# A two-block transformer kernel on one core: gate and up products with the two parts of the input side by side, and the norm's factors on GpSimd

## The chip, the cores and the metric

The program runs on one core of one Trainium2 chip. The metric is the device time of one execution in microseconds (us); the medians of several executions are compared.

## The reference, cut to what matters

Twelve stages work on a residual of 256 tokens by 1024 features in float32: attention of several kinds, a recurrent and a retention mixer, cross attention, and, six times, a SwiGLU feed-forward layer. Each stage is

```
x = x + rms_norm(stage(rms_norm(x, g_pre)), g_post)
swiglu(x, w_gate, w_up, w_down) = (silu(x @ w_gate) * (x @ w_up)) @ w_down     # 1024 -> 2816 -> 1024
```

The change lies in the six feed-forward stages, in the two products with `w_gate` and `w_up`.

## The kernel before

**Products in parts.** TensorE multiplies in fp32r. To keep float32 accuracy each operand is split: `whi` is the weight rounded to fp32r (ScalarE, `act_hi`, L304) and `wlo = raw - whi` (VectorE, `dve_lo`, L311); `xh` and `xl` are the two parts of the normed input, feature-major, `[128, 8, 256]` each. A product is the sum of three: `whi*xh`, `whi*xl`, `wlo*xh` (`mm3`, L243 to L245 and, by operand order, L250 to L252).

**The weight stream.** All weights come as 301 chunks of 128x2048 floats (1 MB each) through three slots: SyncE loads `raw` slot j when the `wlo` of the chunk that was there is done (`w_lo`), ScalarE makes `whi` when TensorE has used the slot (`w_used`), VectorE makes `wlo` when `whi` is there (`w_hi`). In chunk c's body both are made for chunk c+3. One chunk of gate and up holds a 128-column tile of each.

**A feed-forward stage** has 22 chunks of gate and up and 11 of the down product. `slices_pe` (L633, L639) does chunks 0 and 1 while the residual still comes in; `proj_pe` does 20 chunks of 48 products of 256 columns into one of three PSUM banks `pj` (gate in columns 0 to 255, up in the rest). The norm's factors (one for each token, `rP`) are applied behind the product:

- VectorE, for each chunk: L882 `GU = pj * rP` (frees the bank, `pj_free`); `dve_lo`; L887 `A = (TH + 1) * gate`; L890 `M = A * up / 2`; L893, the low part of M.
- ScalarE, for each chunk: `act_hi`; L905 `TH = tanh(gate / 2)`; L907, the high part of M (`own(c)`, `hi2`).
- GpSimd has no part in it; it works a few small operations between stages, and some in the attention of stages 0 and 9.

`GU`, `TH`, `A` and `M` have one buffer each, and each engine takes its instructions strictly in the order written. The down product (L250 to L252, 512 columns) begins behind chunk 21. The bodies of chunks 2 and on run in hardware loops of three chunks (`chunk_loop`). The PSUM banks `acc` hold the transposed residual at the start of a stage and the down product's sums at its end; between the two they are free.

Of the kernel before, what the change touches and what calls it, by code (L numbers as in the profile page):

```python
# [8 lines left out]
P = 128  # L9
D = 1024  # L10
T = 256
# [72 lines left out]
def build_program(nc, stages, wstream, xin, xtok, memin, memtok, vecs_d, gains_d, consts_d, rpb, small, out):  # L84
    NCH = n_chunks(stages)
    with ExitStack() as ctx:
# [5 lines left out]
        def sem(name):  # L92
            if name not in sems:
# [4 lines left out]
        NORM = {"sq": 2, "hi": KT, "lo": KT, "mv": 1, "rs": 1, "bc": 1, "rb": 1}  # L98
        attn = lambda units, groups, H=1: {**{n: units for n in ("s", "sm", "pn", "pt", "pts", "pv")}, "p": H * units,
                                           "od": groups}  # L100
        ADDS = {"ffn": {n: FT for n in ("th", "a", "m", "hi2", "lo2")}, "na": {**attn(8, 8, 4), "oh": 8},
                "dil": {**attn(16, 8, 2), "oh": 8, "pt": 32, "pts": 32}, "xa": {**attn(4, 4, 2), "oh": 4}, "dsa": attn(8, 8, 2), "rwrt": {}}
        base, count = {}, {}

# [21 lines left out]

        xt = sb("xt", [P, 2, D])
        x_at = nc.sbuf_base
        xh = sb("xh", [P, KT, T], F32R)
        xl = sb("xl", [P, KT, T], F32R)  # L130
        sb("space", [P, 16])
        raw = sb("raw", [P, 3, CHUNK])
        w_at = nc.sbuf_base
# [724 lines left out]


        def ffn(tag, s, nxt):  # L860
            sh = FS - KT * T - 5 * T
            GU = F0[:, sh:sh + 512]
            TH = F0[:, sh + 512:sh + 768]
            A = F0[:, sh + 768:sh + 1024]
            M = F0[:, sh + 1024:sh + 1280]

            def own(c):
                return AR[:, c, :] if isinstance(c, int) else AR[:, bass.ds(c, 1), :].rearrange("p o t -> p (o t)")

            def pe_f(pe, w):  # L870
                def tiles(c, j, bank, slot):
                    tile_fm(bank, 0, slot)
                    return tile_fm(bank, 1, slot)
                slices_pe(pe, w)
                proj_pe(pe, w, 1, tiles)
                proj_pe(pe, w, FT - 3, tiles)
                out_pe(pe, w, FT, FT, tag, "lo2", nxt, alternate=True)

            def dve_f(dve, w):
                def body(c, g, gs, it, p, ps):  # L880
                    dve.wait_ge(w_used, g + 1)
                    nc.vector.tensor_tensor(GU.rearrange("p (a t) -> p a t", a=2),  # L882
                                            pj[ps][:, :].rearrange("p (a t) -> p a t", a=2),
                                            rP[:, None, :].to_broadcast([P, 2, T]), ALU.mult).then_inc(pj_free, 1)
                    dve_lo(dve, g, gs)
                    dve.wait_ge(*at(tag, "th", c + 1))
                    nc.vector.scalar_tensor_tensor(A, TH, 1.0, GU[:, 0:T], ALU.add, ALU.mult)\  # L887
                        .then_inc(sg(tag, "a"), 1)
                    dve.wait_ge(*at(tag, "a", c + 1))
                    nc.vector.scalar_tensor_tensor(M, A, 0.5, GU[:, T:2 * T], ALU.mult, ALU.mult)\  # L890
                        .then_inc(sg(tag, "m"), 1)
                    dve.wait_ge(*at(tag, "hi2", c + 1))
                    nc.vector.tensor_tensor(own(c + FT), M, own(c).bitcast(F32), ALU.subtract)\  # L893
                        .then_inc(sg(tag, "lo2"), 1)
                chunk_loop(dve, w, FT, body, peel=2, is_proj=True)
                out_dve(dve, w, FT)

            def act_f(act, w):
                def body(c, g, gs, it, p, ps):
                    if not isinstance(c, int) or c != 1:  # L900
                        act_hi(act, g, gs, it, c)
                    if isinstance(c, int) and c == 0:
                        act_hi(act, g + 1, (g + 1) % 3, (g + 1) // 3, c)
                    act.wait_ge(pj_free, p + 4)
                    nc.scalar.activation(TH, GU[:, 0:T], ACT.Tanh, scale=0.5).then_inc(sg(tag, "th"), 1)  # L905
                    act.wait_ge(*at(tag, "m", c + 1))
                    nc.scalar.activation(own(c), M, ACT.Copy).then_inc(sg(tag, "hi2"), 1)  # L907
                chunk_loop(act, w, FT, body, peel=2, is_proj=True)
                out_act(act, w, s, FT)
            return pe_f, dve_f, act_f  # L910


        mem_hi, mem_lo = AR[:, 16:24, :], AR[:, 24:32, :]
# [61 lines left out]
        def mixer(tag, kind, s, nxt):  # L975
# [267 lines left out]

            def load(sp):
                if na:
                    sp.dma_start(MK, c_dram("na_mask")).then_inc(Mx("tm"), 16)
                    sp.dma_start(NB[:, 0, :], rpb[0, :, :]).then_inc(Mx("tl0"), 16)
                else:
                    sp.dma_start(DM.rearrange("p a n -> p (a n)"), c_dram("dist")).then_inc(Mx("tl"), 16)

            def pool_f(gp):
                if not na:
                    return
                def made(x, n):
                    x.then_inc(Mx("made"), 1)
                    gp.wait_ge(Mx("made"), n)

                def masked(ps_):
                    gp.wait_ge(Mx(f"tl{ps_}"), 16)
                    b = NB[:, ps_, :].rearrange("p (a c) -> p a c", c=T)  # L1260
                    made(nc.gpsimd.tensor_tensor(b, b, MK[:, None, :].to_broadcast([P, 4, T]), ALU.add), BIASED[ps_])

                def mixed(ps_):
                    VB = VBs[ps_ % 3]
                    gp.wait_ge(pj_free, 3 + NCP * (ps_ + 1))
                    if ps_ == 3:
                        gp.wait_ge(*at(tag, "pv", 2))
                    moves = ((1, 3, slice(0, 32)), (1, 0, slice(32, 64)), (1, 0, slice(64, 128)),
                             (2, 3, slice(0, 64)), (2, 3, slice(64, 96)), (2, 0, slice(96, 128)))
                    for n, (i, j, rows) in enumerate(moves):  # L1270
                        made(nc.gpsimd.tensor_copy(VB[rows, :, i, :], VB[rows, :, j, :]), MIXED[ps_] - 5 + n)

                gp.wait_ge(Mx("tm"), 16)
                masked(0)
                masked(1)
                mixed(0)
                mixed(1)
                masked(2)
                mixed(2)
                masked(3)  # L1280
                mixed(3)
# [1467 lines left out]
        @block.scalar  # L2749
        def _(act):  # L2750
            w = Walk()
            act.wait_ge(sem("power"), 1)
            nc.scalar.activation(rsc[:, 0:1], power[:, 0:1], ACT.Copy)
            act.wait_ge(sem("in_vecs"), 16)
            for i in range(2):
                act.wait_ge(x_in[i], 16)
                for k in range(4 * i, 4 * i + 4):
                    pre_hi(act, "s0pre", "na0_pre", False, k)
                act.wait_ge(w_raw[i], 16)
                nc.scalar.activation(whi[:, i, :], raw[:, i, :], ACT.Copy).then_inc(w_hi, 1)  # L2760
            act.wait_ge(x_in[2], 16)
            pre_sq(act, "s0pre")
            act.wait_ge(w_raw[2], 16)
            nc.scalar.activation(whi[:, 2, :], raw[:, 2, :], ACT.Copy).then_inc(w_hi, 1)
            for s, kind, idx, fns in plan:
                fns[2](act, w)
                post_act(act, w, f"s{s}post", out_banks(kind))
                if s + 1 < len(plan):
                    nx = plan[s + 1]
                    pre_act(act, w, f"s{s + 1}pre", f"{nx[1]}{nx[2]}_pre", nx[1] == "dil")  # L2770
                    if len(nx[3]) > 3:
                        nx[3][3](act)

        @block.vector
        def _(dve):
            w = Walk()
            nc.vector.memset(AR[:, 0:2, :].bitcast(F32), 0.0).then_inc(sem("zeroed"), 1)
            nc.vector.memset(nt[:, :], 0.0).then_inc(pj_free, 3)
            dve.wait_ge(pj_free, 3)
            dve.wait_ge(sem("in_vecs"), 16)  # L2780
            for i in range(2):
# [21 lines left out]
        @block.gpsimd  # L2803
        def _(gp):
            nc.gpsimd.memset(power[:, :], -0.5).then_inc(sem("power"), 1)
            gp.wait_ge(sem("power"), 1)
            stats_pool(gp, "s0pre", rsc[:, 2:4], 8)
            for s, kind, idx, fns in plan:
                if kind == "dsa":
                    gp.wait_ge(sem(f"s{s}_mv"), 1)  # L2810
                    nc.gpsimd.tensor_tensor(nt[:, 8:12], nt[:, 0:4], power[:, 0:4], ALU.pow)\
                        .then_inc(sem(f"s{s}_rs"), 1)
                    fns[4](gp)
                if kind in ("rwrt", "na"):
                    fns[4](gp)
                if kind in ("dsa", "rwrt"):
                    mem_pool(gp, f"s{s + 1}m")
                post_pool(gp, f"s{s}post")
                if s + 1 < len(plan):
                    stats_pool(gp, f"s{s + 1}pre", rsc[:, 2:4], 8)  # L2820

        @block.tensor
        def _(pe):
# [4 lines left out]
                for _ in range(n):  # L2828
                    nc.tensor.matmul(mb[:, 0:T], AR[:, 0, 0:P], AR[:, 1, :], start=True, stop=True)

            pe.wait_ge(sem("zeroed"), 1)
            pe.wait_ge(x_in[0], 16)
            warm(26)
            pe.wait_ge(sem("in_cst"), 16)
# [206 lines left out]
```

## Time and profile before

| | us |
|---|---|
| median of 3 runs | 1929.08 (1928.88 to 1930.92) |
| the profiled execution, its own time | 1927.48 |
| its span | 1925.7 |
| granted TensorE clock, mean | 0.995 |

The span is what the rows below are read from; 1.8 us of the execution lie around it. Engines: PE is TensorE, DVE VectorE, ACT ScalarE, POOL GpSimd. A busy share is over the whole span and mixes all stages.

### The profile page before, as it was taken

Reading aid. Unit: us, or ns where it says so; the run is one execution under the profiler, and the core shown is the slowest. Engines: PE = TensorE matmul, PEld = TensorE weight load, DVE = VectorE, ACT = ScalarE, POOL = GpSimd, SP = SyncE. Lnnn points to the kernel's source line nnn. Section 1 sums busy time; section 2 is a strip of 40 time slices with the busy share of each in tenths; the row PEclk is TensorE's granted clock in tenths of the full one; section 3 lists DMA queues with packets and bytes.
Section 4 is the critical chain, followed back from the end, with each engine's and each line's share of the span. In section 5 each row is a group of like instructions: output and inputs, shape, how many; then the busy total and the mean of one; then the engine's idle time right before and its main releaser. Section 6 shows DMA issues by size and latency. Waiting matters only on the chain.

```text
span 1925.7 us, 38585 instructions
## 1 busy us (share of the span) xinstructions
PE 1864.5 (97%) x15800; PEld 1761.9 (91%) x15800; DVE 1339.8 (70%) x1814; ACT 920.9 (48%) x1255; POOL 85.0 (4%) x104
## 2 busy tenths in 40 slices
PE   8999999999989999999999999999999999899998
PEld 8989989999979998999998888999899988799997
DVE  6867756766777775776677677777577667677774
ACT  5554445444454444444436454444444444555442
POOL 2300000000000000000000010000000003100000
PEclk9999999999999999999999999999999999999999
DMA  7445564443525564556541223556455652354553
GB/s 293 154 165 197 185 237 183 176 177 132 182 93 187 186 229 174 188 183 233 216 173 53 112 94 148 189 185 228 174 191 183 234 206 110 121 186 153 177 204 131
DMA packets 50099, 338.13 MB, mean 176 GB/s; under 512 B 6080, under 2 KB 7232, under 8 KB 10560
## 3 DMA queue, kind: packets, MB, share of 16 engines
q1 hardware_dynamic: 45072, 319.74, 45.8%
q10 hardware_dynamic: 4912, 16.71, 2.4%
q8 instruction: 90, 1.47, 0.3%
q14 instruction: 25, 0.20, 0.0%
HBM read 335.38 MB, written 1.05 MB: 175 GB/s over the span
## 4 chain that ended last, share of the span: by engine, by line
PE 62%; DVE 13%; ACT 11%; issue 9%; POOL 1%; ACTq 1%; DVEq 0%; POOLq 0%
PE pj L243 9%; PE pj L245 9%; PE pj L244 9%; ACT whi L304 9%; PE acc L250 5%; PE acc L251 5%; PE acc L252 5%; DVE wlo L311 4%; PE pj L633 3%; PE pj L250 2%; PE pj L251 2%; PE pj L252 2%; PE pj L639 2%; DVE F L890 2%; DVE F L887 1%
## 5 line engine op out<-in xcount | busy, mean ns | idle before, releaser
L311 DVE TENSOR_TENSOR wlo<-raw,whi 128x2048 fp32r<-128x2048 f32 x285 | 651.8, 2291 | 238.8 <-ACT whi L304 237.7
L243 PE MATMUL pj<-xh,whi 128*128 128x256 f32 x2672 | 739.7, 277 | 1.3 <-DVE wlo L311 0.5
L244 PE MATMUL pj<-xl,whi 128*128 128x256 f32 x2672 | 734.8, 275 | 0.0
L245 PE MATMUL pj<-xh,wlo 128*128 128x256 f32 x2672 | 734.8, 275 | 0.0
L304 ACT ACTIVATE whi<-raw 128x2048 fp32r<-128x2048 f32 x298 | 567.9, 1912 | 331.2 <-PE acc L252 142.8
L243 PEld LDWEIGHTS pj<-xh,whi 128*128 128x128 f32 x2672 | 512.8, 192 | 6.3 <-issue 2.2
L245 PEld LDWEIGHTS pj<-xh,wlo 128*128 128x128 f32 x2672 | 513.0, 192 | 0.0
L244 PEld LDWEIGHTS pj<-xl,whi 128*128 128x128 f32 x2672 | 512.9, 192 | 0.1
L250 PE MATMUL acc<-whi,AR 128*128 128x512 f32 x656 | 253.9, 387 | 3.8 <-DVE AR L1449 3.3
L251 PE MATMUL acc<-whi,AR 128*128 128x512 f32 x656 | 249.6, 381 | 0.0
L252 PE MATMUL acc<-wlo,AR 128*128 128x512 f32 x656 | 249.4, 380 | 0.0
L907 ACT ACTIVATE AR<-F 128x256 f32 (+1 forms) x132 | 55.2, 418 | 375.3 <-DVE F L890 375.3
L250 PEld LDWEIGHTS acc<-whi,AR 128*128 128x128 f32 x656 | 128.3, 196 | 24.8 <-DVE wlo L311 7.1
L252 PEld LDWEIGHTS acc<-wlo,AR 128*128 128x128 f32 x656 | 128.4, 196 | 14.1
L251 PEld LDWEIGHTS acc<-whi,AR 128*128 128x128 f32 x656 | 128.4, 196 | 13.1
L893 DVE TENSOR_TENSOR AR<-F,AR 128x256 f32 (+1 forms) x132 | 56.2, 426 | 101.4 <-ACT AR L907 101.4
L882 DVE TENSOR_TENSOR F<-pj,rP 128x512 f32<-128x512 f32 x132 | 90.5, 686 | 1.4
L250 PE MATMUL pj<-whi,xh 128*128 128x256 f32 x288 | 80.2, 279 | 1.8 <-issue 1.7
L633 PE MATMUL pj<-xh,whi 128*128 128x256 f32 x320 | 80.1, 288 | 0.1
L251 PE MATMUL pj<-whi,xl 128*128 128x256 f32 x288 | 79.2, 275 | 0.0
L252 PE MATMUL pj<-wlo,xh 128*128 128x256 f32 x288 | 79.2, 275 | 0.0
L633 PE MATMUL pj<-xh,wlo 128*128 128x256 f32 x320 | 76.0, 275 | 0.0
(398 smaller groups left out, 2196.3 us busy)
## 6 DMA issues: line engine op xcount, KB each, us to landing
raw<-in_wstream SPq DMA_DIRECT2D x301, 1024.0 KB, 4.8
F<-in_gains ACTq DMA_DIRECT2D x12, 512.0 KB, 4.3
XM<-in_memtok ACTq DMA_DIRECT2D x2, 1024.0 KB, 4.9
XM<-in_memin ACTq DMA_DIRECT2D x2, 1024.0 KB, 7.8
F<-in_rpb ACTq DMA_DIRECT2D x3, 512.0 KB, 3.8
F<-in_small ACTq DMA_DIRECT2D x1, 1536.0 KB, 9.4
F<-in_xin SPq DMA_DIRECT2D x2, 512.0 KB, 6.4
xt<-in_xtok SPq DMA_DIRECT2D x1, 1024.0 KB, 11.7
```

Source lines behind the costliest of these rows:

```text
L243: nc.tensor.matmul(o, wh, k_hi, start=first, stop=False, skip_group_check=True)
L244: nc.tensor.matmul(o, wh, k_lo, start=False, stop=False, skip_group_check=True)
L245: return nc.tensor.matmul(o, wl, k_hi, start=False, stop=last, skip_group_check=True)
L250: nc.tensor.matmul(o, k_hi, wh, start=first, stop=False, skip_group_check=True)
L251: nc.tensor.matmul(o, k_lo, wh, start=False, stop=False, skip_group_check=True)
L252: return nc.tensor.matmul(o, k_hi, wl, start=False, stop=last, skip_group_check=True)
L304: nc.scalar.activation(whi[:, gs, :], raw[:, gs, :], ACT.Copy).then_inc(w_hi, 1)
L311: nc.vector.tensor_tensor(wlo[:, gs, :], raw[:, gs, :], whi[:, gs, :].bitcast(F32), ALU.subtract).then_inc(w_lo, 1)
L633: nc.tensor.matmul(o, a[:, (w.g + c) % 3, wk], woven(xh[:, k, :]), start=k == 0 and half == 0 and i == 0, stop=False, skip_group_check=True)
L882: nc.vector.tensor_tensor(GU.rearrange("p (a t) -> p a t", a=2), pj[ps][:, :].rearrange("p (a t) -> p a t", a=2), rP[:, None, :].to_broadc ...
L893: nc.vector.tensor_tensor(own(c + FT), M, own(c).bitcast(F32), ALU.subtract)\
L907: nc.scalar.activation(own(c), M, ACT.Copy).then_inc(sg(tag, "hi2"), 1)
```

## The change

For chunks 2 to 19 of each feed-forward stage (18 of 22), with `xh` and `xl` now neighbours in one tile `xhl`:

- TensorE multiplies each `whi` block once, with both parts of the input, as one product of 512 columns (128 of them for each half of each part, interleaved as before), and then adds `wlo*xh` in columns 0 to 255. Gate goes to bank `pj[ps]`, up to bank `acc[ps]`; each bank then holds the main sum in columns 0 to 255 and the `whi*xl` sum in columns 256 to 511.
- ScalarE copies the two `whi*xl` sums to `LOW` (two new copies of 256 columns, ahead of `act_hi`).
- VectorE adds each bank's main sum and `LOW` into `SUM` (two additions of 256 columns in place of the multiplication of 512), and then frees the banks.
- GpSimd multiplies `SUM` by `rP` into `GU` (one operation of 512 columns, both inputs in SBUF) and signals `gu`; tanh waits for that.
- `dve_lo` in these bodies is that of the chunk before (`g - 1`), so `wlo` of chunk c+2 is made in body c, not that of c+3. Body 20 makes two.

Beside it, two waits on small start-up semaphores are merged into others (`tm` into `tl0`, `zeroed` into `pj_free`).

```diff
+        xhl = sb("xhl", [P, 2, KT, T], F32R)
+        xh, xl = xhl[:, 0, :, :], xhl[:, 1, :, :]
...
+            def wide(c):
+                return not isinstance(c, int) or 2 <= c < FT - 2
...
+                def both_parts(c, g, gs, it, p, ps):
+                    pe.wait_ge(w_lo, g + 1)
+                    pe.wait_ge(pj_free, p + 1)
+                    for half, bank in enumerate((pj[ps], acc[ps])):
+                        for k in range(KT):
+                            wk = slice((half * KT + k) * P, (half * KT + k + 1) * P)
+                            nc.tensor.matmul(bank[:, :], whi[:, gs, wk],
+                                             xhl[:, :, k, :].rearrange("p s (a b) -> p s b a", a=2),
+                                             start=k == 0, stop=False, skip_group_check=True)
+                            last = nc.tensor.matmul(bank[:, 0:T], wlo[:, gs, wk], woven(xh[:, k, :]),
+                                                    start=False, stop=k == KT - 1, skip_group_check=True)
+                    last.then_inc(w_used, 1)
                 slices_pe(pe, w)
-                proj_pe(pe, w, 1, tiles)
-                proj_pe(pe, w, FT - 3, tiles)
+                chunk_loop(pe, w, FT - 4, both_parts, peel=3, is_proj=True)
+                proj_pe(pe, w, 2, tiles)
+                pe.wait_ge(pj_free, 3 + p0 + FT - 2)
...
             def dve_f(dve, w):
                 def body(c, g, gs, it, p, ps):
                     dve.wait_ge(w_used, g + 1)
-                    nc.vector.tensor_tensor(GU..., pj..., rP..., ALU.mult).then_inc(pj_free, 1)
-                    dve_lo(dve, g, gs)
+                    if wide(c):
+                        dve.wait_ge(*at(tag, "ls", c - 1))
+                        for half, bank in enumerate((pj[ps], acc[ps])):
+                            hh = slice(half * T, (half + 1) * T)
+                            x = nc.vector.tensor_tensor(SUM[:, hh], bank[:, 0:T], LOW[:, hh], ALU.add)
+                        x.then_inc(pj_free, 1)
+                    else:
+                        nc.vector.tensor_tensor(GU..., pj..., rP..., ALU.mult).then_inc(pj_free, 1)
+                    if wide(c) or c == FT - 2:
+                        dve_lo(dve, g - 1, (gs + 2) % 3)
+                    if not wide(c) and c != 1:
+                        dve_lo(dve, g, gs)
...
             def act_f(act, w):
                 def body(c, g, gs, it, p, ps):
+                    if wide(c):
+                        act.wait_ge(w_used, g + 1)
+                        for half, bank in enumerate((pj[ps], acc[ps])):
+                            x = nc.scalar.activation(LOW[:, half * T:(half + 1) * T], bank[:, T:2 * T], ACT.Copy)
+                        x.then_inc(sg(tag, "ls"), 1)
...
-                    act.wait_ge(pj_free, p + 4)
+                    if wide(c):
+                        act.wait_ge(*at(tag, "gu", c - 1))
+                    else:
+                        act.wait_ge(pj_free, p + 4)
...
+            def pool_f(gp):
+                def body(c, g, gs, it, p, ps):
+                    gp.wait_ge(pj_free, 3 + p0 + 2 + c + 1)
+                    nc.gpsimd.tensor_tensor(GU..., SUM..., rP..., ALU.mult).then_inc(sg(tag, "gu"), 1)
+                chunk_loop(gp, Walk(), FT - 4, body)
```

## Rows read from the trace of the kernel before

**Rows 1.** The page: span, and each engine's busy time, share and instructions.
```profile
span 1925.7 us, 38585 instructions
...
PE 1864.5 (97%) x15800; PEld 1761.9 (91%) x15800; DVE 1339.8 (70%) x1814; ACT 920.9 (48%) x1255; POOL 85.0 (4%) x104
```

**Rows 2.** Timeline of TensorE, first feed-forward stage: start, duration, engine, line.
```profile
135.62 0.38 PE L243 MATMUL pj<-xh,whi 128*128 128x256 f32 x1
...
171.24 0.28 PE L243 MATMUL pj<-xh,whi 128*128 128x256 f32 x1
...
173.91 0.28 PE L243 MATMUL pj<-xh,whi 128*128 128x256 f32 x1
...
243.25 0.49 PE L250 MATMUL acc<-whi,AR 128*128 128x512 f32 x1
...
245.73 0.38 PE L252 MATMUL acc<-wlo,AR 128*128 128x512 f32 x1
...
248.32 0.38 PE L252 MATMUL acc<-wlo,AR 128*128 128x512 f32 x1
248.72 0.49 PE L250 MATMUL acc<-whi,AR 128*128 128x512 f32 x1
```

**Rows 3.** Timeline of VectorE, one chunk of the same stage and the next one's beginning.
```profile
167.84 0.68 DVE L882 TENSOR_TENSOR F<-pj,rP 128x512 f32<-128x512 f32 x1
168.96 2.29 DVE L311 TENSOR_TENSOR wlo<-raw,whi 128x2048 fp32r<-128x2048 f32 x1 [0.44 <-ACT whi L304]
171.17 0.42 DVE L887 SCALAR_TENSOR_TENSOR F<-F 128x256 f32<-128x256 f32 x1
171.62 0.42 DVE L890 SCALAR_TENSOR_TENSOR F<-F 128x256 f32<-128x256 f32 x1
172.85 0.43 DVE L893 TENSOR_TENSOR AR<-F,AR 128x256 f32 x1 [0.80 <-ACT AR L907]
173.19 0.68 DVE L882 TENSOR_TENSOR F<-pj,rP 128x512 f32<-128x512 f32 x1
```

**Rows 4.** Timeline of ScalarE, the same stage: the seam between two bodies, twice.
```profile
172.17 0.42 ACT L907 ACTIVATE AR<-F 128x256 f32 x1 [2.95 <-DVE F L890]
172.50 1.90 ACT L304 ACTIVATE whi<-raw 128x2048 fp32r<-128x2048 f32 x1
...
177.64 0.42 ACT L907 ACTIVATE AR<-F 128x256 f32 x1 [2.94 <-DVE F L890]
178.15 1.92 ACT L304 ACTIVATE whi<-raw 128x2048 fp32r<-128x2048 f32 x1
```

**Rows 5.** Groups by shape: a ScalarE copy of 256 columns out of PSUM.
```profile
L2639 ACT ACTIVATE PTb<-pj 128x256 f32<-128x256 f32 x5 | 1.9, 384 | 0.4
```

**Rows 6.** Timeline of GpSimd and of VectorE where both work, two places.
```profile
19.97 2.37 POOL L1261 TENSOR_TENSOR F<-F 128x1024 f32<-128x1024 f32 x1 [1.01 <-DMA F<-in_rpb]
...
20.20 4.28 DVE L321 TENSOR_TENSOR wlo<-raw,whi 128x2048 fp32r<-128x2048 f32 x1 [2.09 <-ACT whi L2764]
...
1641.93 1.82 POOL L1868 TENSOR_TENSOR F<-F 128x256 f32<-128x256 f32 x1
...
1641.95 1.22 DVE L317 TENSOR_TENSOR wlo<-raw,whi 128x1024 fp32r<-128x1024 f32 x1
```

**Rows 7.** One line of GpSimd: count, shortest, median and longest in ns.
```profile
L1868 POOL TENSOR_TENSOR F<-F x4: 730/732/1816, 1623.5 to 1641.9; 128x256 f32<-128x256 f32 x4
```

**Rows 8.** The page's DMA issues: KB each, median us to landing.
```profile
raw<-in_wstream SPq DMA_DIRECT2D x301, 1024.0 KB, 4.8
```

**Rows 9.** TensorE in stage 9: its timeline, then a window with its granted clock.
```profile
1647.66 0.56 PE L716 MATMUL acc<-cst,Sb 128*128 128x128 f32 x2 [1.91 <-DVE Sb L770]
...
1648.00:1650.00 2.00, 2.00 (x11) 0.50 0.82 315
```

More of the change, by code:

```diff
@@ L100, in build_program @@
                                            "od": groups}
-        ADDS = {"ffn": {n: FT for n in ("th", "a", "m", "hi2", "lo2")}, "na": {**attn(8, 8, 4), "oh": 8},
+        ADDS = {"ffn": {**{n: FT for n in ("th", "a", "m", "hi2", "lo2")}, "gu": FT - 4, "ls": FT - 4}, "na": {**attn(8, 8, 4), "oh": 8},
                 "dil": {**attn(16, 8, 2), "oh": 8, "pt": 32, "pts": 32}, "xa": {**attn(4, 4, 2), "oh": 4}, "dsa": attn(8, 8, 2), "rwrt": {}}
@@ L128, in build_program @@
         x_at = nc.sbuf_base
-        xh = sb("xh", [P, KT, T], F32R)
-        xl = sb("xl", [P, KT, T], F32R)
+        xhl = sb("xhl", [P, 2, KT, T], F32R)
+        xh, xl = xhl[:, 0, :, :], xhl[:, 1, :, :]
         sb("space", [P, 16])
@@ L860, in ffn @@
         def ffn(tag, s, nxt):
[L861 to L865, printed above, removed]
+            sh = FS - KT * T - 9 * T
+            SUM = F0[:, sh:sh + 512]
+            GU = F0[:, sh + 512:sh + 1024]
+            TH = F0[:, sh + 1024:sh + 1280]
+            A = F0[:, sh + 1280:sh + 1536]
+            M = F0[:, sh + 1536:sh + 1792]
+            LOW = F0[:, sh + 1792:sh + 2304]
+            p0 = sum(proj_chunks(kind_) for kind_, _ in stages[:s])
             def own(c):
                 return AR[:, c, :] if isinstance(c, int) else AR[:, bass.ds(c, 1), :].rearrange("p o t -> p (o t)")
+            def wide(c):
+                return not isinstance(c, int) or 2 <= c < FT - 2
             def pe_f(pe, w):
+                assert w.p == p0
                 def tiles(c, j, bank, slot):
@@ L881, in body @@
                     dve.wait_ge(w_used, g + 1)
-                    nc.vector.tensor_tensor(GU.rearrange("p (a t) -> p a t", a=2),
-                                            pj[ps][:, :].rearrange("p (a t) -> p a t", a=2),
-                                            rP[:, None, :].to_broadcast([P, 2, T]), ALU.mult).then_inc(pj_free, 1)
-                    dve_lo(dve, g, gs)
+                    if wide(c):
[5 more added lines that the diff above has]
+                    else:
+                        nc.vector.tensor_tensor(GU.rearrange("p (a t) -> p a t", a=2),
+                                                pj[ps][:, :].rearrange("p (a t) -> p a t", a=2),
+                                                rP[:, None, :].to_broadcast([P, 2, T]), ALU.mult).then_inc(pj_free, 1)
+                    if wide(c) or c == FT - 2:
+                        dve_lo(dve, g - 1, (gs + 2) % 3)
+                    if not wide(c) and c != 1:
+                        dve_lo(dve, g, gs)
                     dve.wait_ge(*at(tag, "th", c + 1))
@@ L909, in act_f @@
                 out_act(act, w, s, FT)
-            return pe_f, dve_f, act_f
+            def pool_f(gp):
+                def body(c, g, gs, it, p, ps):
+                    gp.wait_ge(pj_free, 3 + p0 + 2 + c + 1)
+                    nc.gpsimd.tensor_tensor(GU.rearrange("p (a t) -> p a t", a=2), SUM.rearrange("p (a t) -> p a t", a=2),
+                                            rP[:, None, :].to_broadcast([P, 2, T]), ALU.mult).then_inc(sg(tag, "gu"), 1)
+                chunk_loop(gp, Walk(), FT - 4, body)
+            return pe_f, dve_f, act_f, None, pool_f
         mem_hi, mem_lo = AR[:, 16:24, :], AR[:, 24:32, :]
@@ L1245, in load @@
                 if na:
-                    sp.dma_start(MK, c_dram("na_mask")).then_inc(Mx("tm"), 16)
+                    sp.dma_start(MK, c_dram("na_mask")).then_inc(Mx("tl0"), 16)
                     sp.dma_start(NB[:, 0, :], rpb[0, :, :]).then_inc(Mx("tl0"), 16)
@@ L1258, in masked @@
                 def masked(ps_):
-                    gp.wait_ge(Mx(f"tl{ps_}"), 16)
+                    gp.wait_ge(Mx(f"tl{ps_}"), 16 if ps_ else 32)
                     b = NB[:, ps_, :].rearrange("p (a c) -> p a c", c=T)
@@ L1271, in mixed @@
                         made(nc.gpsimd.tensor_copy(VB[rows, :, i, :], VB[rows, :, j, :]), MIXED[ps_] - 5 + n)
-                gp.wait_ge(Mx("tm"), 16)
                 masked(0)
@@ L2770, in _ @@
                     pre_act(act, w, f"s{s + 1}pre", f"{nx[1]}{nx[2]}_pre", nx[1] == "dil")
-                    if len(nx[3]) > 3:
+                    if len(nx[3]) > 3 and nx[3][3]:
                         nx[3][3](act)
@@ L2776, in _ @@
             w = Walk()
-            nc.vector.memset(AR[:, 0:2, :].bitcast(F32), 0.0).then_inc(sem("zeroed"), 1)
-            nc.vector.memset(nt[:, :], 0.0).then_inc(pj_free, 3)
+            nc.vector.memset(AR[:, 0:2, :].bitcast(F32), 0.0).then_inc(pj_free, 1)
+            nc.vector.memset(nt[:, :], 0.0).then_inc(pj_free, 2)
             dve.wait_ge(pj_free, 3)
@@ L2813, in _ @@
                     fns[4](gp)
-                if kind in ("rwrt", "na"):
+                if kind in ("rwrt", "na", "ffn"):
                     fns[4](gp)
@@ L2829, in warm @@
                     nc.tensor.matmul(mb[:, 0:T], AR[:, 0, 0:P], AR[:, 1, :], start=True, stop=True)
-            pe.wait_ge(sem("zeroed"), 1)
+            pe.wait_ge(pj_free, 3)
             pe.wait_ge(x_in[0], 16)
```

## The prediction

> **What bounds the kernel now.** I read the page's first part, then the timelines of the four engines inside one feed-forward stage. On the page TensorE is busy 97% of the span, VectorE 70%, GpSimd 4% [rows 1]: TensorE's time is the kernel's time, and GpSimd looks free. The timelines qualify this. TensorE runs chunks 2 to 21 from 135.62 to 243.25, 107.63 us or 5.38 a chunk, without a visible gap [rows 2]. VectorE and ScalarE form a closed ring beside it: `act_hi` is queued behind `own(c)`, `dve_lo` needs `act_hi`, A and M follow, and `own(c+1)` needs M. From one L907 to the next it is 172.17 to 177.64, 5.47 us [rows 4], a little more than TensorE's chunk; the three-deep buffers absorb the difference until the down product, where TensorE waits about 0.2 us for a weight's low part (248.32 to 248.72, against a step of 0.216) [rows 2]. So two things decide what the change is worth: TensorE's columns, and whether the ring, which it lengthens, still fits.
>
> **TensorE's part.** Inside a chunk 24 products of 256 columns take 171.24 to 173.91, 0.1113 each; 12 of 512 take 245.73 to 248.32, 0.2158 each [rows 2]. A wide chunk has 16 products of 512 and 16 of 256 in place of 48 of 256: it saves 16 x (0.2226 - 0.2158) = 0.11 us and takes 5.38 - 0.11 = 5.27. Over 18 x 6 = 108 chunks that is 11.8 us at most; nothing, if the interleaved wide product costs twice the narrow one. The Trainium skill (TensorE: Matmul & The Clock Gate, "Back-to-back issue gap") gives columns / 2.4 + 2.5 ns, which is 109.2 and 215.8 ns: the trace agrees at 512 and not at 256, and by the page the saving would be an estimated 4.5 us. Neither enters the sum below, because there TensorE isn't what is late.
>
> **The ring after the change.** The program order on each engine now makes one loop: ScalarE copies LOW (c+1) only behind `own(c)`, VectorE adds only behind LOW, GpSimd multiplies behind the additions, tanh waits for GpSimd, A for tanh, M for A, `own` for M. I add it up from the start of `own`:
>
> - `own` to the first copy 0.33 (172.17 to 172.50) [rows 4]; second copy 0.33 later; it lasts 0.38 [rows 5], and with 0.04 for the hand-over the first addition starts at 1.08. VectorE itself is ready at 1.02 (0.68 to L893, 0.34 more to the next) [rows 3], so it isn't later.
> - Additions of 256 columns: no longer than the 0.42 of the other 256-column operations, next start after 0.34 [rows 3]. Second addition 1.42 to 1.84; `dve_lo`, which waits for nothing now, starts at 1.76 and lasts 2.29, to 4.05.
> - GpSimd is released at 1.84, starts at about 1.90, and finds VectorE's L311 running. What then happens is the heart of this prediction. At 20.20 the VectorE subtraction (two SBUF inputs, elsewhere 2.29 [rows 3]) took 4.28 while GpSimd's 2.37 us operation from 19.97 was under way: it ended 2.14 after GpSimd did. At 1641.93 a GpSimd operation that otherwise takes 0.73 [rows 7] took 1.82 beside a VectorE subtraction of the same kind, and ended 0.58 behind it [rows 6]. So the one that comes second does practically all its work after the other's end, except some 0.15 us. That is no slow-down in proportion but an exclusion. The Trainium skill says the same (SBUF — State Buffer, "SBUF: two separate sides"): the port pair shared by VectorE and GpSimd is locked for the whole instruction by whoever starts first, where VectorE reads two SBUF inputs and GpSimd reads SBUF. The trace agrees with its 4.28 and 1.82. It is the rule that speaks against this change.
> - GpSimd's price for 512 columns: from 256 at 0.73 [rows 7] and 1024 at 2.37 [rows 6] a line gives 1.28; the bounds are half the large one, 1.19, and twice the small one, 1.46. Behind the lock it ends at 4.05 + 1.28 - 0.15 = 5.18.
> - tanh at 5.23, 0.40 long; A at 5.66; M 0.45 later; `own` 0.55 after M (171.62 to 172.17) [rows 3, 4]: 6.66. The hardware loop's branch adds 0.18 every third chunk (0.51 against 0.33) [rows 4], 0.06 on average: 6.72.
>
> The ring takes 6.72 us, TensorE's wide chunk 5.27. TensorE will idle 1.45 us in each.
>
> **One stage.** Count from 0, TensorE's start of chunk 2 (135.62 in the trace). Chunk 2 ends at 5.27, LOW and the additions begin (first addition 6.08), and `dve_lo` of chunk 4 ends at 9.05. From there the low part of chunk h, without which TensorE doesn't begin it, comes at 9.05 + 6.72 (h - 4): chunk 21 starts at 9.05 + 17 x 6.72 = 123.3. The down product needs `wlo` of chunk 22, made in body 20: `own(19)` is 2.61 after that start, L882 1.02 more, the subtraction some 0.6 behind L882 and 2.29 long, 6.5 in all (TensorE is through with chunk 21 at 5.38 and waits). The down product starts at 129.8, against 107.63 before: +22.2, less the 0.2 that TensorE waited there before, which the body's second `dve_lo` now covers. That is +22.0 us a stage, +132 for six.
>
> Costed at nothing: `act_hi` (1.9) lies under the wait for GpSimd; if that wait went it would still lie under `dve_lo`. The weight loads are asked for one body later, since SP waits for `w_lo`; the load for chunk c+3 is issued at the end of `dve_lo` in body c-2 and used at `act_hi` in body c, 2 x 6.72 - 3.05 = 10.4 us later, and takes 4.8 [rows 8]. Behind GpSimd's new wait nothing is queued until the stage's end (`post_pool`). The merged start-up semaphores: two waits, under 0.1 us either way. The `acc` banks are free in these chunks; the wait ahead of the down product is for an addition two chunks old.
>
> **Sum.** 1927.5 + 132 = 2059.5 for the profiled execution; that lies 1.6 below the median of 1929.1, so the median comes to 2061, 6.8% slower.
>
> **Rivals.**
>
> - *GpSimd comes first.* If the wait on `w_hi` holds `dve_lo` back by 0.2 us, GpSimd takes 1.90 to 3.18, and `dve_lo` ends 2.14 later, at 5.32; tanh is then covered, `own` follows at 6.24, with the branch 6.30. Stage: 6.08 + 4.24 + 17 x 6.30 + 5.4 = 122.8, +15.2, or +91 in all: 2020. Against it: VectorE starts the next instruction 0.34 behind a 0.42 us one [rows 3], ahead of its semaphore. Chance 0.13.
> - *No exclusion (the other side: faster).* If VectorE and GpSimd overlap, GpSimd is done at 3.18 and tanh before `dve_lo` ends; A at 3.97, M 4.42, `own` 4.97, with the branch 5.03, below 5.27. TensorE sets the pace, 0.11 us less a chunk, and its small wait goes: -13, 1916. It decides once the ring falls under about 5.4; the exclusion is worth 1.7 of 6.72, so nearly all of it has to be absent. For it: the rows of the exclusion are of other shapes, and GpSimd's are rough. Chance 0.11.
> - *No exclusion, and the interleaved wide product costs two narrow ones.* No gain: 1929. Chance 0.05.
> - *The clock.* TensorE fell to its lower level (granted 0.50) after 1.91 us of idling [rows 9]. The gaps here are 1.45, of a kind that repeats. One fall in each stage costs about 5.27 - 1.45 = 3.8 us, or 23 in all (2084); one in every third chunk 36 x 3.8 = 137 (2198). Against it: it lasted two windows and the gap before was longer. Chance 0.08.
>
> **The numbers.** The forecast has 0.63. Its own range: GpSimd at 1.19 or 1.46 moves the ring by -0.09 or +0.18, and 0.05 more on each of four hand-overs whose register waits I could not read adds 0.2; 17 x 6 rings make that -9 to +39: 2052 to 2100. With GpSimd first (2020, and its own bound of -9) and single falls of the clock inside, 2010 to 2105 holds about 8 in 10. A difference of 0.2% is about what the runs can tell from no change. Faster by more than that 0.11, within it 0.06, slower 0.83.
>
> **What would show it.** In the changed profile: L311 at 2.29 and, beside it, GpSimd's new line at about 3.3 us each (1.28 if there is no exclusion), or, with GpSimd first, GpSimd at 1.28 and L311 at 3.5; tanh's idle time ended by GpSimd; the period of a VectorE addition 6.7; TensorE waiting 1.4 us a chunk for `wlo` and its busy share down to about 91%; products of 512 in a step of 0.216; no change in other stages. I am wrong if the period is 5.3 with GpSimd's line short, and wrong in size if the period is right but TensorE's clock row shows half levels, or if the GpSimd line takes well over 1.5 net of the lock.

## The result, and the profile after

The changed kernel takes 2062.81 us (median of 4 runs, 2061.72 to 2064.42) against 1929.16 before: a ratio of 1.0691, 95% interval 1.0673 to 1.071. It is 6.9% slower; the forecast was 2061.

The page of the changed kernel, beside [rows 1]; PE is TensorE, DVE VectorE, ACT ScalarE. The last two lines are from its list of costly groups (engine, operation, output and inputs, shape, count | busy us, mean ns | idle time before it and what ended it):

```profile
span 2060.8 us, 35796 instructions
...
PE 1871.9 (91%) x14072; PEld 1702.4 (83%) x14072; DVE 1348.4 (65%) x1922; ACT 991.7 (48%) x1471; POOL 436.0 (21%) x212
...
PE 43%; issue 29%; POOL 12%; DVE 8%; ACT 3%; POOLq 0%; ACTq 0%; DVEq 0%
...
L955 POOL TENSOR_TENSOR F<-F,rP 128x512 f32<-128x512 f32 x108 | 351.1, 3251 | 422.9 <-DVE F L909 422.9
L889 PE MATMUL pj<-xhl,whi 128*128 128x512 f32 x864 | 298.8, 393 | 110.1 <-DVE wlo L311 109.8
```

TensorE's busy time barely moved (1864.5 to 1871.9), while its share fell from 97% to 91%: of the 135 us of span, 128 are idling of TensorE. The wide product's line now waits 109.8 us for VectorE's low part, where TensorE's lines before waited for next to nothing, and GpSimd, which had no part in the feed-forward stages, carries 12% of the chain that ended last (the chain is followed back from the last instruction of the run). No engine is full. What grew is a chain through several of them.

That chain can be read off three timelines of one chunk. GpSimd first, then VectorE (beside [rows 3]), then ScalarE (beside [rows 4]):

```profile
165.61 3.25 POOL L955 TENSOR_TENSOR F<-F,rP 128x512 f32<-128x512 f32 x1 [3.63 <-DVE F L909]
172.36 3.25 POOL L955 TENSOR_TENSOR F<-F,rP 128x512 f32<-128x512 f32 x1 [3.50 <-DVE F L909]
```

```profile
164.78 0.43 DVE L909 TENSOR_TENSOR F<-pj,F 128x256 f32<-128x256 f32 x1 [0.21 <-ACT F L936]
165.12 0.41 DVE L909 TENSOR_TENSOR F<-acc,F 128x256 f32<-128x256 f32 x1
165.45 2.28 DVE L311 TENSOR_TENSOR wlo<-raw,whi 128x2048 fp32r<-128x2048 f32 x1
169.34 0.43 DVE L920 SCALAR_TENSOR_TENSOR F<-F 128x256 f32<-128x256 f32 x1 [1.61 <-ACT F L946]
169.80 0.43 DVE L923 SCALAR_TENSOR_TENSOR F<-F 128x256 f32<-128x256 f32 x1
171.18 0.43 DVE L926 TENSOR_TENSOR AR<-F,AR 128x256 f32 x1 [0.95 <-ACT AR L948]
171.53 0.42 DVE L909 TENSOR_TENSOR F<-pj,F 128x256 f32<-128x256 f32 x1
```

```profile
168.89 0.42 ACT L946 ACTIVATE F<-F 128x256 f32<-128x256 f32 x1 [2.50 <-POOL F L955]
170.37 0.42 ACT L948 ACTIVATE AR<-F 128x256 f32 x1 [1.06 <-DVE F L923]
170.69 0.37 ACT L936 ACTIVATE F<-pj 128x256 f32<-128x256 f32 x1
```

The reader is to see one thing: the subtraction L311 starts at 165.45 and ends at 167.73, with its usual 2.28; GpSimd's product starts at 165.61, 0.16 later, and ends at 168.86, that is 1.13 behind the subtraction. It does not run beside it. tanh (L946) starts 0.03 after GpSimd's end, A (L920) when tanh is done, M, the high part (L948), and only then ScalarE's copies (L936) for the next chunk. VectorE stands idle for 1.61 us in the middle of its own ring. From the first `dve_lo` of the stage, at 144.83, to that of body 19, at 259.71, there are 17 periods of 6.76 us (forecast 6.72). The other five feed-forward stages run a little faster, 6.65 to 6.67 us from addition to addition; over all six the mean is 6.67. Why the first is slower stays open.

### The profile page after: what moved, and what is told of

Read it like the earlier page. It is cut to its first block, busy times and chain, and to the rows that moved or that the text cites. A ratio compares the mean times of both kernels' runs of the same rounds, so it can differ in the third digit from the quotient of the medians.

```text
span 2060.8 us, 35796 instructions
## 1 busy us (share of the span) xinstructions
PE 1871.9 (91%) x14072; PEld 1702.4 (83%) x14072; DVE 1348.4 (65%) x1922; ACT 991.7 (48%) x1471; POOL 436.0 (21%) x212
## 3 DMA queue, kind: packets, MB, share of 16 engines
q8 instruction: 92, 1.51, 0.3%
## 4 chain that ended last, share of the span: by engine, by line
PE 43%; issue 29%; POOL 12%; DVE 8%; ACT 3%; POOLq 0%; ACTq 0%; DVEq 0%
POOL F L955 11%; PE acc L250 6%; PE acc L252 6%; PE acc L251 6%; PE pj L243 4%; PE pj L245 4%; PE pj L244 4%; DVE wlo L311 2%; PE pj L250 2%; PE pj L252 2%; PE pj L251 2%; ACT whi L304 1%; PE pj L633 1%; PE mb L729 1%; PE acc L703 1%
## 5 line engine op out<-in xcount | busy, mean ns | idle before, releaser
L311 DVE TENSOR_TENSOR wlo<-raw,whi 128x2048 fp32r<-128x2048 f32 x285 | 650.8, 2288 | 188.5 <-ACT whi L304 187.7
L955 POOL TENSOR_TENSOR F<-F,rP 128x512 f32<-128x512 f32 x108 | 351.1, 3251 | 422.9 <-DVE F L909 422.9
L889 PE MATMUL pj<-xhl,whi 128*128 128x512 f32 x864 | 298.8, 393 | 110.1 <-DVE wlo L311 109.8
L889 PEld LDWEIGHTS pj<-xhl,whi 128*128 128x128 f32 x864 | 163.0, 189 | 159.2 <-issue 132.8
L889 PE MATMUL acc<-xhl,whi 128*128 128x512 f32 x864 | 288.8, 382 | 0.0
L243 PE MATMUL pj<-xhl,whi 128*128 128x256 f32 x944 | 264.6, 280 | 12.9 <-DVE wlo L311 12.8
L244 PE MATMUL pj<-xhl,whi 128*128 128x256 f32 x944 | 259.7, 275 | 0.0
L245 PE MATMUL pj<-xhl,wlo 128*128 128x256 f32 x944 | 259.6, 275 | 0.0
L892 PE MATMUL acc<-xhl,wlo 128*128 128x256 f32 x864 | 235.5, 273 | 0.0
L892 PE MATMUL pj<-xhl,wlo 128*128 128x256 f32 x864 | 235.5, 273 | 0.0
L243 PEld LDWEIGHTS pj<-xhl,whi 128*128 128x128 f32 x944 | 181.2, 192 | 19.0 <-DVE wlo L311 15.9
L946 ACT ACTIVATE F<-F 128x256 f32<-128x256 f32 x132 | 54.8, 415 | 266.6 <-POOL F L955 260.1
L889 PEld LDWEIGHTS acc<-xhl,whi 128*128 128x128 f32 x864 | 163.3, 189 | 22.8
L245 PEld LDWEIGHTS pj<-xhl,wlo 128*128 128x128 f32 x944 | 181.4, 192 | 0.0
L244 PEld LDWEIGHTS pj<-xhl,whi 128*128 128x128 f32 x944 | 181.3, 192 | 0.1
L368 POOL TENSOR_TENSOR rsc<-ss,power 128x1 f32<-128x1 f32 x24 | 13.2, 551 | 778.4 <-DVE ss L457 778.4
L920 DVE SCALAR_TENSOR_TENSOR F<-F 128x256 f32<-128x256 f32 x132 | 56.1, 425 | 177.3 <-ACT F L946 177.3
L892 PEld LDWEIGHTS acc<-xhl,wlo 128*128 128x128 f32 x864 | 165.9, 192 | 0.0
```

What stands on the lines that cost most here:

```text
L243: nc.tensor.matmul(o, wh, k_hi, start=first, stop=False, skip_group_check=True)
L244: nc.tensor.matmul(o, wh, k_lo, start=False, stop=False, skip_group_check=True)
L245: return nc.tensor.matmul(o, wl, k_hi, start=False, stop=last, skip_group_check=True)
L311: nc.vector.tensor_tensor(wlo[:, gs, :], raw[:, gs, :], whi[:, gs, :].bitcast(F32), ALU.subtract).then_inc(w_lo, 1)
L889: nc.tensor.matmul(bank[:, :], whi[:, gs, wk], xhl[:, :, k, :].rearrange("p s (a b) -> p s b a", a=2), start=k == 0, stop=False, skip_grou ...
L892: last = nc.tensor.matmul(bank[:, 0:T], wlo[:, gs, wk], woven(xh[:, k, :]), start=False, stop=k == KT - 1, skip_group_check=True)
```

## The experiments

Each ratio is against runs of the kernel before that were taken beside the experiment, on the same chip: 1929.9 us for the first four experiments, 1930.0 for the next three, 1926.9 for the last two.

**GpSimd's product and the subtraction in series.**

```diff
+                    if wide(c):
+                        dve.wait_ge(*at(tag, "gu", c - 1))
                     if wide(c) or c == FT - 2:
                         dve_lo(dve, g - 1, (gs + 2) % 3)
```

> The changed kernel, with VectorE's subtraction (L311) in the 18 wide bodies made to wait for GpSimd's product. GpSimd and the subtraction no longer meet. Exclusion theory: GpSimd takes 1.28 us, its price alone (in the changed kernel 3.25, beside the subtraction), and the ring is 1.84 to the second addition's end, 3.18 to GpSimd's end, A at 5.43, own at 6.43, 6.49 with the branch, so shorter than the 6.75 now although the two are in series: 1929 + 110 = about 2039 us. Rival, GpSimd is simply slow on this shape (3.25 by itself): the ring grows by another 2 us, to about 8.4, and the time to about 2240 us.

Measured 2057.81 (ratio 1.0662, 1.0631 to 1.0693). All of GpSimd's products of this kernel (count, shortest, median and longest in ns):

```profile
L957 POOL TENSOR_TENSOR F<-F,rP x108: 1276/1293/1312, 145.2 to 1983.5; 128x512 f32<-128x512 f32 x108
```

Alone the operation takes 1.29 us, never over 1.31; in the changed kernel all 108 lie between 3.25 and 3.27. The slow-GpSimd rival is out. Putting the two strictly one behind the other costs nothing against letting them "overlap" (2057.8 against 2062.8), which is what exclusion means. The time missed my 2039 by 19: the ring here is 6.57 on average and not 6.49 (the subtraction starts 0.13 after GpSimd's end), some 8 us over 102 periods, and the stage's start was mis-sized (below), about 13 more, less some 4 in the down product. That leaves 2 open.

**The subtraction with one SBUF input.** Same place, same 2048 columns, but the second input lies in PSUM. The low weight parts of these chunks are then not the right ones; only the time is of use.

```diff
-                    if wide(c) or c == FT - 2:
+                    if wide(c):
...
+                        nc.vector.tensor_tensor(v8(wlo), v8(raw), mb[:, None, 0:T].to_broadcast([P, 8, T]),
+                                                ALU.subtract).then_inc(w_lo, 1)
+                    if not wide(c) and c == FT - 2:
                         dve_lo(dve, g - 1, (gs + 2) % 3)
```

> The changed kernel, with one thing other: in the 18 wide bodies the second input of VectorE's subtraction is not whi in SBUF but a PSUM bank that nobody writes there (a broadcast of 256 columns), so the operation has one SBUF input, the same 2048 columns and the same place. The low weight parts of those chunks are thus not the right ones; everything else is as in the changed kernel. Exclusion theory: GpSimd 1.28 us beside the subtraction, the ring 5.03, under TensorE's chunk of 5.27, so TensorE sets the pace and the time is about 1916 us, faster than before the change. Rival, the ring is long because of its steps and GpSimd's own slowness: GpSimd stays at 3.25 and the time near 2062 us. Second rival, the engines share bandwidth in proportion whatever the inputs: GpSimd 2 us or more, the ring 5.8 or more, above 1960 us.

Measured 1916.0 (ratio 0.9927, 0.9898 to 0.9956). Its VectorE and its GpSimd:

```profile
170.53 2.28 DVE L919 TENSOR_TENSOR wlo<-raw,mb 128x2048 fp32r<-128x2048 f32 x1
172.73 0.42 DVE L926 SCALAR_TENSOR_TENSOR F<-F 128x256 f32<-128x256 f32 x1
```

```profile
170.70 1.30 POOL L961 TENSOR_TENSOR F<-F,rP 128x512 f32<-128x512 f32 x1 [3.62 <-DVE F L909]
```

This is the experiment that decides. The VectorE operation has the same length and the same start relative to GpSimd's (0.17 before it), and now they overlap fully: GpSimd takes 1.30, A follows the subtraction without a gap. 147 us of the changed kernel's time hang on where one operand lies. It also shows that the rest of the change (copies, additions, later weights) fits under TensorE when the exclusion is gone: from the middle of each stage on, its bodies follow each other at TensorE's pace, 5.24 us.

The edit changes two things about the second input, its memory and its pattern (a block of 256 columns read eight times). The kernel before tells them apart in stage 9, where VectorE works beside GpSimd with plain patterns:

```profile
1628.41 0.69 DVE L1754 SCALAR_TENSOR_TENSOR F<-F 128x512 f32<-128x512 f32 x1
1628.70 0.98 POOL L1867 TENSOR_TENSOR F<-F 128x256 f32<-128x256 f32 x1
...
1639.12 0.76 DVE L1548 SCALAR_TENSOR_TENSOR F<-pj,F 128x256 f32<-128x256 f32 x2 [0.62 <-PE pj L703]
1639.29 0.73 POOL L1865 TENSOR_TENSOR F<-F 128x256 f32<-128x256 f32 x1
```

Beside L1754, with both inputs in SBUF, GpSimd's 0.73 becomes 0.98 and ends 0.58 behind VectorE; beside L1548, with one input in PSUM, it stays 0.73. So the memory is enough to explain the difference.

**The factors on VectorE, GpSimd idle.**

```diff
+                        dve.wait_ge(pj_free, p + 4)
+                        nc.vector.tensor_tensor(GU..., SUM..., rP..., ALU.mult).then_inc(sg(tag, "gu"), 1)
...
-            return pe_f, dve_f, act_f, None, pool_f
+            return pe_f, dve_f, act_f
```

> The changed kernel, with the multiplication by the norm's factors done by VectorE (512 columns, 0.69 us) behind the additions; GpSimd idle. Exclusion theory: the ring loses GpSimd's 1.13 us behind the subtraction and the wait for tanh, and gains 0.63 on VectorE: A at 4.68, own 5.68, 5.74 with the branch; 5 us a stage above before, about 1958 us. Rival, the ring is not what sets the pace (the lost time lies on TensorE's side, in the weights coming one body later): the time stays near 2062 us.

Measured 1963.13 (ratio 1.0171, 1.0142 to 1.0201). VectorE is busier than in the changed kernel (72% against 65%) and the kernel is 100 us faster: 0.69 us of VectorE's own work in the ring is cheaper than 1.13 us of waiting for a lock plus the tanh that then has no cover. From one L311 to the next it is 5.66 and 5.88, 5.71 on average over the six stages (expected 5.74).

**TensorE's part undone.**

```diff
-                            nc.tensor.matmul(bank[:, :], whi[:, gs, wk], xhl[:, :, k, :]...)
+                            nc.tensor.matmul(bank[:, 0:T], whi[:, gs, wk], woven(xh[:, k, :]), ...)
+                            nc.tensor.matmul(bank[:, T:2 * T], whi[:, gs, wk], woven(xl[:, k, :]), ...)
```

> The changed kernel, with only TensorE's part undone: each wide product of 512 columns is two of 256 again, into the same columns of the same banks, 5.38 us of TensorE a chunk in place of 5.27. Ring theory: TensorE idles 1.4 us in each chunk and the time doesn't move, 2062 to 2063 us. Rival, TensorE's columns count in part: up to 12 us more, 2074 us.

Measured 2065.72 (2065.47 and 2065.97), 2.9 above the changed kernel, whose runs were taken at another time. By the profile a feed-forward stage takes the same (from GpSimd's post-norm of stage 2 to that of stage 3: 594.15 to 798.46, 204.3 us, against 594.88 to 799.14, 204.3); the difference lies in stages 5 and 9 (2.0 and 1.8 us longer), which the edit doesn't touch and which vary as much between executions of the other kernels. The wide product earns nothing here.

**TensorE's part alone,** with the rings as before; the `whi*xl` sums are computed and left out of the result.

```diff
+                            x = nc.vector.tensor_tensor(GU[:, hh], bank[:, 0:T], rP[:, :], ALU.mult)
...
+                    dve_lo(dve, g, gs)
```

> TensorE's part of the change alone: wide products, but VectorE multiplies the two banks' main sums by the factors directly (two operations of 256 columns for one of 512, the same 0.68 us), ScalarE copies nothing, GpSimd is idle, and the subtraction is that of chunk c+3, as before the change. The whi*xl sums of the 18 chunks are computed and left out of the result. Ring theory: the old ring of VectorE and ScalarE (5.47 us plus the branch, 5.53) was already longer than TensorE's 5.38, and the down product's start waits for the subtraction of body 19, so a shorter TensorE chunk gains nothing or nearly: 1927 to 1930 us. Rival, TensorE alone set the pace before: 108 x 0.11 = 12 us less, 1917 us.

Measured 1928.87 (ratio 0.9998, 0.9987 to 1.0010). No gain at all. Its ScalarE, with nothing added:

```profile
167.07 0.42 ACT L936 ACTIVATE AR<-F 128x256 f32 x1 [2.96 <-DVE F L919]
...
172.53 0.42 ACT L936 ACTIVATE AR<-F 128x256 f32 x1 [2.94 <-DVE F L919]
```

5.46 us from body to body, as in [rows 4], and 5.54 on average with the loops' branches. The old ring was already a little longer than TensorE's chunk, and it, not TensorE, sets when the down product's weights are ready.

**A shorter ring for the same arithmetic.** VectorE applies the factors and splits the subtraction; the second half fills the time in which ScalarE makes the high part.

```diff
+                        (the factors on VectorE, as above)
-                    if wide(c) or c == FT - 2:
-                        dve_lo(dve, g - 1, (gs + 2) % 3)
-                    if not wide(c) and c != 1:
-                        dve_lo(dve, g, gs)
+                    dve.wait_ge(w_hi, g + 4)
+                    half_lo(dve, gs, 0)
...
                         .then_inc(sg(tag, "m"), 1)
+                    half_lo(dve, gs, 1).then_inc(w_lo, 1)
                     dve.wait_ge(*at(tag, "hi2", c + 1))
```

> A version that keeps the whole arithmetic of the change, without GpSimd and with a shorter ring: VectorE adds, multiplies by the factors, does half of the subtraction, A and M, then the other half of the subtraction while ScalarE makes the high part, then the low part; the subtraction is again that of chunk c+3. Ring: own, two copies 0.33 and 0.27, act_hi to 2.8, half a subtraction 1.14, A, M, own: 4.97, with the branch 5.03, under TensorE's 5.27. Theory: TensorE sets the pace, 108 x 0.11 us less and the small waits at the start of the down product gone: 1914 to 1918 us. Rival, TensorE's narrow chunk is not the bound or the wide product's gain of 0.0068 us each doesn't hold in this loop: 1925 to 1930 us. Rival, VectorE's own load (about 4.9 us of 5.27 a chunk) doesn't fit with its register waits: 1930 to 1945 us.

Measured 1908.76 (ratio 0.9892, 0.9874 to 0.9910): 1.1% faster than before the change and 7.5% faster than the change. One body of its VectorE:

```profile
169.79 0.42 DVE L909 TENSOR_TENSOR F<-pj,F 128x256 f32<-128x256 f32 x1
170.12 0.41 DVE L909 TENSOR_TENSOR F<-acc,F 128x256 f32<-128x256 f32 x1
170.57 0.69 DVE L912 TENSOR_TENSOR F<-F,rP 128x512 f32<-128x512 f32 x1
171.32 1.23 DVE L317 TENSOR_TENSOR wlo<-raw,whi 128x1024 fp32r<-128x1024 f32 x1
172.47 0.42 DVE L921 SCALAR_TENSOR_TENSOR F<-F 128x256 f32<-128x256 f32 x1
172.92 0.42 DVE L924 SCALAR_TENSOR_TENSOR F<-F 128x256 f32<-128x256 f32 x1
173.26 1.22 DVE L317 TENSOR_TENSOR wlo<-raw,whi 128x1024 fp32r<-128x1024 f32 x1
174.40 0.42 DVE L928 TENSOR_TENSOR AR<-F,AR 128x256 f32 x1
174.75 0.42 DVE L909 TENSOR_TENSOR F<-pj,F 128x256 f32<-128x256 f32 x1
```

4.96 us, and practically without idling, under TensorE's 5.27. Late in each stage TensorE sets the pace and the bodies follow each other at 5.24. It beat its forecast by 5 us.

**The kernel before, with the split alone.**

```diff
-                    dve_lo(dve, g, gs)
+                    dve.wait_ge(w_hi, g + 4)
+                    half_lo(dve, gs, 0)
...
+                    half_lo(dve, gs, 1).then_inc(w_lo, 1)
```

> The kernel before, with the subtraction in the gate and up bodies split in two, the second half between M and the low part. The ring falls from 5.53 to about 4.4, TensorE's products are as before. Theory: TensorE already ran without gaps up to the down product; only the waits for low parts at its start (0.2 to 0.5 us a stage) go: 1926 to 1928.5 us. Rival, the old ring cost more than that: below 1925 us.

Measured 1922.51 (ratio 0.9967, 0.9954 to 0.9979), 7.5 us faster, which is the rival's side of what I had expected (below 1925). By its profile a feed-forward stage takes about 1.0 us less (first stage, from 119.03 to 299.48, 180.45, against 118.72 to 300.22, 181.50), six of them 5.8. Nearly all of it is the down product: in that stage of the kernel before, TensorE waits at several of its steps for 0.9 us in all, and here at none, where I had expected 0.2 to 0.5. The rest lies in stages without an edit and is not explained. In the version above a stage takes 178.3 (stage 3, 566.75 to 745.02), against 180.4 with the split alone (569.62 to 750.03): the wide products bring 2.1 us a stage, 18 x 0.11 = 2.0 by the step rates of [rows 2]. So TensorE's saving is real, and needs the short ring to be seen.

**GpSimd back in the short ring.** The version with the split, its factors on GpSimd as in the change.

```diff
-                    if wide(c) or c == FT - 2:
-                        dve_lo(dve, g - 1, (gs + 2) % 3)
...
+                    half_lo(dve, gs, 0)
...
+                    half_lo(dve, gs, 1).then_inc(w_lo, 1)
```

> The version with the split subtraction (1908.8 us, e6_split_lo), but with the factors applied by GpSimd again as in the change. Here VectorE's first half of the subtraction waits for ScalarE's act_hi (2.8 us into the ring), so GpSimd's product (1.9 to 3.2) starts first and meets only its first 0.4 us. Exclusion theory, whoever starts first holds the port: GpSimd 1.28 to 1.31, the first half of the subtraction 1.5 to 1.65 in place of 1.22, A at 4.2, own at 5.2, 5.2 with the branch, just under TensorE's 5.27: 1908 to 1913 us. So GpSimd's product itself would not be what costs, only its place. Rival, GpSimd's product is too slow for this ring wherever it lies: above 1930 us.

Measured 1914.19 (ratio 0.9929, 0.9916 to 0.9942). Its GpSimd, then its VectorE:

```profile
168.04 1.29 POOL L954 TENSOR_TENSOR F<-F,rP 128x512 f32<-128x512 f32 x1 [4.09 <-DVE F L909]
```

```profile
168.75 1.66 DVE L317 TENSOR_TENSOR wlo<-raw,whi 128x1024 fp32r<-128x1024 f32 x1 [0.80 <-ACT whi L304]
...
171.13 1.22 DVE L317 TENSOR_TENSOR wlo<-raw,whi 128x1024 fp32r<-128x1024 f32 x1
```

Now GpSimd holds the port and VectorE's half subtraction is the one stretched, 1.66 against 1.22, ending 1.08 behind GpSimd (over all 108 bodies 1.51 to 1.75, always 1.07 to 1.09 behind). The ring is 5.38, a little over TensorE's 5.27, and the time a little over the 1908 to 1913 expected: GpSimd started 2.08 and not 1.90 into the ring. GpSimd's product is not the mistake; queueing it behind a 2.3 us subtraction was. It still is slower than VectorE doing it (ratio 0.9929 against 0.9892; their intervals just don't meet, and the runs were taken at different times).

**One thing undone: the subtraction of chunk c+3.**

```diff
-                    if wide(c) or c == FT - 2:
-                        dve_lo(dve, g - 1, (gs + 2) % 3)
-                    if not wide(c) and c != 1:
-                        dve_lo(dve, g, gs)
+                    dve_lo(dve, g, gs)
```

> The change with one thing undone: body c again makes the low part of chunk c+3 (whose high part ScalarE makes in the same body), in place of that of c+2, so that the whole subtraction starts behind act_hi, at 2.8 in the ring, when GpSimd already holds the port (1.9 to 3.2). This is the order of the rival in which GpSimd comes first. Exclusion theory: GpSimd 1.28 to 1.31, L311 about 2.6 from its start in place of 2.29, ending at 5.3; A 5.24, own 6.24, the ring 6.30 against 6.75; the down product starts about 12 us later than before the change in each stage and not 25: about 2000 us. Rival, the order of the two does not matter to the ring, only their sum: near 2060 us.

Measured 2009.21 (ratio 1.0425, 1.0407 to 1.0443). L311 takes 2.47 to 2.70 here and ends 2.15 behind GpSimd, GpSimd takes 1.29, and the ring is 6.27 from one high part to the next, 6.29 on average. The time is 9 above the 2000 that I expected: in the first stage the down product starts 14.3 us later than before the change, and not 12. So the order matters: the move of `dve_lo` to the chunk before, which looks like relief for VectorE (it waits for nothing), is what let it win the port, and accounts for some 50 of the 134 us.

## Why the prediction was right

**The exclusion,** read from two chance encounters in stages 0 and 9 [rows 6], carried over to another shape. I had GpSimd's line at about 3.3 beside the subtraction; it is 3.25. The tail behind the subtraction, 1.28 - 0.15 = 1.13, is 1.13. The one-input experiment shows the cause. One thing the prediction passed over: in the second encounter GpSimd's record starts 0.02 us before VectorE's (1641.93 against 1641.95), and GpSimd is the one that waits. So "who starts first" can't be read from records that close; it held where the starts lie at least 0.16 us apart (GpSimd 0.16 behind in the changed kernel, 0.23 ahead in stage 0, 0.61 to 0.97 ahead in the last two experiments). The Trainium skill (SBUF — State Buffer, "SBUF: two separate sides") has the same rule, and what it says of two SBUF inputs held here: they locked out GpSimd (3.25), and with one of them in PSUM GpSimd ran free (1.30). The same section names a second case, a VectorE operation in a 2-port performance mode, which the prediction left out. Two SBUF inputs are indeed not the whole condition; this is the kernel before in stage 0:

```profile
58.08 2.39 POOL L1261 TENSOR_TENSOR F<-F 128x1024 f32<-128x1024 f32 x1
58.33 2.22 DVE L770 TENSOR_SCALAR F<-F,sm 128x128 f32<-128x128 f32 x1
```

L770 scales one SBUF tile by a factor for each row, and takes 0.28 us by itself; behind GpSimd it took 2.22 and ended 0.08 after it. No run shows in which mode it ran.

**The order** was VectorE first, as forecast. The rival with GpSimd first describes the last experiment, with a ring of 6.29 where I had 6.30; its 2020 us were 11 too many.

**The ring,** 6.72 forecast, is 6.76 in the first stage, where its parts agree within 0.1, and 6.67 on average over the six. **TensorE** idles 1.1 to 1.6 us before nearly every wide chunk, and a body takes 6.67 - 5.24 = 1.43 us more than TensorE's part of it (forecast 1.45), and its share is 91% as said. The wide product and the narrow one behind it take what [rows 2] gave for 512 and 256 columns. The rule of the Trainium skill that gave a smaller saving (TensorE: Matmul & The Clock Gate, "Back-to-back issue gap") is off at 256 columns here: the saving measured between the two split versions is 2.1 us a stage and more, 13.2 over the six by the profiles, not 4.5.

**The clock** stayed: the granted clock is 1.00 in every stretch of 10 us of the first feed-forward stage's wide chunks, and the profiled run's mean is 0.997. So gaps of 1.1 to 1.6 us that come back with every chunk didn't lower it. The fall to 0.50 in [rows 9] comes after a gap of 1.91; that the gap's length makes the difference is not shown, since TensorE's work around it is another.

**Three terms were mis-sized, in opposite directions.** The stage's start: I let the first addition follow TensorE's chunk 2, at 6.08. It came at 144.16, which is 8.24 after TensorE's start at 135.92 (8.24 or 8.25 in all six stages), since ScalarE is still at chunks 0 and 1 until then:

```profile
135.23 3.71 ACT L304 ACTIVATE whi<-raw 128x2048 fp32r<-128x2048 f32 x2 [4.51 <-PE pj L639]
...
143.16 0.42 ACT L948 ACTIVATE AR<-F 128x256 fp32r<-128x256 f32 x1 [0.95 <-DVE F L923]
143.49 0.36 ACT L936 ACTIVATE F<-pj 128x256 f32<-128x256 f32 x1
```

That is 2.2 us a stage too little, 13 in all. Against that stand two others. The ring is 0.05 shorter than forecast on average, 5 us over its 102 periods. And the down product of before waited for 0.9 us, not for the 0.2 that I took from its first seam; in the changed kernel 0.1 is left, which makes 4 us in all. The slower ring is not what ends these waits: the last experiment, with a ring of 6.29 and the old order of the subtractions, waits for 0.85 again. The one thing it undoes is the order, so the order ends them.

The first stage is the one with the longest ring: its down product starts 132.7 after TensorE's chunk 2 (268.61 - 135.92), +25.1 against before and not +22.2, and from end to end (GpSimd's post-norm, 118.72 to 300.22 before, 119.01 to 324.74 after) it costs +24.2. The six stages together cost +137 by the profiles, forecast +132. The span grew by only 135.1, because the recurrent stage (stage 5) was 2.4 us shorter in this execution; it lies between 202.0 and 206.5 us in all the profiles, whatever the kernel. The median's hit within 2 us is thus partly luck; the mechanism and the ring are not.

**What the prediction saw and did not use:** that the old ring was longer than TensorE's chunk. I wrote -13 for the case without exclusion, and that holds (1916.0 measured, 1916 forecast) only because that ring, with the subtraction moved, is 5.0 (4.9 to 5.1 in most bodies where it sets the pace). With the old ring the same products gain nothing.

## What to carry to other kernels

Before moving an elementwise operation from VectorE to an idle GpSimd, look what VectorE runs at that moment: an operation with two SBUF inputs shuts GpSimd out until its end, and the reverse. With one input in PSUM it did not; with its one tile in SBUF it can still wait, as L770 did. Add up the closed ring of in-order engines, not their busy shares; the change was lost with no engine above 91%. To gain from a cheaper TensorE chunk, first shorten the ring beside it: here, splitting one 2.3 us operation, so that its second half covers another engine's answer, made both kinds of gain visible.

## What the runs showed of the hardware that had not been expected

How exact the exclusion is: 108 products from 3.247 to 3.266 us, each ending 1.13 to 1.15 after the subtraction; in the reverse order VectorE's halves always end 1.07 to 1.09 behind GpSimd. And that a PSUM operand in place of an SBUF one, with the duration unchanged at 2.28, removes it entirely.
